# Neighbourhood attention's queries and keys projected in turned form and as two float32r parts, with the transposes one round later and two score tiles ahead of hyena's turns

## What is computed

```python
h = modulate_2(rmsnorm(x, g_mix), sh1, sc1)
z = h @ w_in[i]                                   # 256 x 3072
q, k, v = jnp.split(z[..., 3 * C_HYENA:], 3, axis=-1)   # 512 columns each, 16 heads of 32
hc = modulate_2(rmsnorm(xc, g_mix), csh1, csc1)   # the context, 256 tokens
kc, vc = jnp.split(hc @ w_in[i][:, kv_off:], 2, axis=-1)
y_na = neighborhood_attention(to_grid(q), to_grid(k), to_grid(v), kc, vc, na_rpb[i])
y_hy = hyena_mixer(z[..., :3 * C_HYENA], *hy)     # short filter, then two long convolutions
x = x + gt1 * (jnp.concatenate([y_hy, y_na], axis=-1) @ w_mix_out[i])
```

## Time and profile before

| what | value |
|---|---|
| runs | median 2493.89 us of 3, 2490.82 to 2494.59 |
| the profiled execution, its own time | 2489.44 us |
| its span | 2488.1 us |
| TensorE busy | 2369.3 us, 95% of the span |
| VectorE, ScalarE, GpSimd busy | 1788.6, 1223.7, 402.8 us |
| granted TensorE clock, mean | 0.968 of full |
| the projection (first L2491 to the end of L2497) | 898.7 to 1017.2 us |
| turns, attention and convolution | 1019.75 to 1152.9 us |

### The profile page before, as it was taken

How to read it: one execution, slowest core, us unless ns; L and a number is a source line. 1 busy time by engine, 2 the same in 40 slices (tenths; PEclk the granted TensorE clock), 3 DMA queues, 4 the chain that set the end, 5 groups by cost and what they waited for, 6 DMA issues and landing times.

```text
span 2488.1 us, 27394 instructions
## 1 busy us (share of the span) xinstructions
PE 2369.3 (95%) x10947; PEld 1770.0 (71%) x10949; DVE 1788.6 (72%) x2022; ACT 1223.7 (49%) x1441; POOL 402.8 (16%) x446
## 2 busy tenths in 40 slices
PE   6987999999999999899999989999999999999998
PEld 2455798544589875454997658778787788788886
DVE  4755577585688755455675358888888898889897
ACT  1132553223155321222443257676767777777775
POOL 1234470132247010253120000000000000000000
PEclk9988999997999999899999999999999999999999
DMA  7641478632447775104665339989998999899995
GB/s 306 252 180 51 179 275 314 225 147 109 159 179 263 306 297 201 76 6 164 236 221 203 146 139 354 363 326 367 349 368 317 367 344 369 318 363 357 363 355 217
DMA packets 50671, 630.35 MB, mean 253 GB/s; under 512 B 8695, under 2 KB 9384, under 8 KB 12840
## 3 DMA queue, kind: packets, MB, share of 16 engines
q1 hardware_dynamic: 44192, 618.81, 65.8%
q10 hardware_dynamic: 3960, 6.97, 0.9%
q0 software_dynamic: 2384, 2.73, 0.3%
HBM read 624.82 MB, written 3.67 MB: 253 GB/s over the span
## 4 chain that ended last, share of the span: by engine, by line
PE 81%; DVE 10%; DMA 3%; ACT 3%; issue 2%; POOL 1%; ACTq 0%; SPq 0%; DVEq 0%; POOLq 0%
PE psum L1136 18%; PE psum L1137 18%; PE psum L1138 18%; PE psum L1004 5%; PE psum L1031 4%; PE psum L2497 3%; DVE sbuf L701 2%; DVE ring_r L1131 2%; PE psum L2491 2%; DMA ring<-in_t_moe 2%; PE psum L741 1%; PE psum L1220 1%; PE psum L3110 1%; PE psum L1171 1%; DMA ring<-in_t_ada 1%
## 5 line engine op out<-in xcount | busy, mean ns | idle before, releaser
L1137 PE MATMUL psum<-ring_r,sc_r 128*128 128x512 f32 x1688 | 665.7, 394 | 0.0
L1131 DVE TENSOR_TENSOR ring_r<-ring,sbuf_r 128x2048 fp32r<-128x2048 f32 (+1 forms) x287 | 537.0, 1878 | 157.6 <-ACT sbuf_r L1122 156.0
L1122 ACT CAST sbuf_r<-ring 128x2048 fp32r<-128x2048 f32 (+1 forms) x287 | 444.9, 1556 | 327.1 <-PE psum L1138 252.2
L1131 DVE TENSOR_TENSOR ring_r<-ring,sc_r 128x2048 fp32r<-128x2048 f32 (+1 forms) x243 | 476.4, 1972 | 116.6 <-ACT sc_r L1122 116.0
L1122 ACT CAST sc_r<-ring 128x2048 fp32r<-128x2048 f32 (+1 forms) x243 | 397.3, 1642 | 255.6 <-PE psum L1138 216.2
L1136 PE MATMUL psum<-sbuf_r,sc_r 128*128 128x512 f32 (+1 forms) x1148 | 427.0, 372 | 4.5 <-DVE sc L2821 3.4
L1137 PEld LDWEIGHTS psum<-ring_r,sc_r 128*128 128x128 f32 x1688 | 317.3, 188 | 72.1 <-issue 1.4
L701 DVE SCALAR_TENSOR_TENSOR sbuf<-ring,sbuf 128x512 f32<-128x512 f32 x404 | 328.2, 819 | 20.5 <-DMA ring<-in_t_ada 15.0
L1138 PE MATMUL psum<-sbuf_r,sc_r 128*128 128x512 f32 x860 | 340.1, 395 | 0.0
L1136 PE MATMUL psum<-sc_r 128*128 128x512 f32 x828 | 330.9, 400 | 0.0
L1138 PE MATMUL psum<-sc_r 128*128 128x512 f32 x828 | 324.3, 392 | 0.0
(11 more groups left out here) (343 smaller groups left out, 2825.3 us busy)
## 6 DMA issues: line engine op xcount, KB each, us to landing
ring<-in_t_moe SPq DMA_DIRECT2D x168, 2048.0 KB, 7.9
ring<-in_t_ada SPq DMA_DIRECT2D x48, 2048.0 KB, 9.5
ring<-in_t_mlp SPq DMA_DIRECT2D x32, 2048.0 KB, 8.1
ring<-in_t_win SPq DMA_DIRECT2D x17, 2048.0 KB, 9.6
ring<-in_t_ffn SPq DMA_DIRECT2D x16, 2048.0 KB, 8.2
ring<-in_t_out SPq DMA_DIRECT2D x7, 2048.0 KB, 8.6
ring<-in_t_bias SPq DMA_DIRECT2D x2, 2048.0 KB, 10.0
spectra<-sc POOLq DMA_DIRECT2D x5, 512.0 KB, 3.9
```

The costliest lines, as they stand in the source:

```text
L1122: p.act.e.copy(p.r(hi), src).then_inc(*p.sig("high", st.tag, n))
L1131: p.dve.e.tensor_tensor(p.r(src), src, p.r(hi), ALU.subtract).then_inc(*p.sig("lowp", st.tag, n))
L1137: e.matmul(out, l[0], r[1], start=False, stop=False)
```

## The change

Queries and keys (units 6 to 11, tiles 3 and 4) are projected in turned form like hyena's columns, the context's keys too. `put_in2` splits each of these units into two float32r parts: ScalarE writes the rounded (and for queries scaled) part out of PSUM, then VectorE subtracts it from PSUM and writes the rest. The turns of queries and keys and the scaling on VectorE go. A score tile is now three float32r matmuls of 512 columns (high by high, high by low, low by high) where it was two float32 matmuls of 256. The depth of `Heads("na", ...)` goes from 2 to 3. The first two score tiles are made before hyena's turns; VectorE takes the first one's maximum before it copies hyena's turns, and ScalarE the first exponential behind its copies of them. Some buffers move. The loads of `skip` are issued behind the first exponential.

```diff
-        self.QA = v3(sc[:, 11288:12312], 4)
-        self.KA = v3(sc[:, 12312:13336], 4)
-        self.KC = v3(sc[:, 13336:14360], 4)
+
+        self.QAH, self.QAL = (v3(UQ[:, i, 0:1024], 4) for i in range(2))
+        self.KAL = [v3(self.GROW[3], 2), v3(sc[:, 13336:14360], 2)]
@@
-                             [(i,) for i in range(3)], [(3,), (4,)], 2)
+                             [(i,) for i in range(3)], [(3,), (4,)], 3)
@@
-                q = self.QA[r0:r0 + 32, h // 4, 128 * b:128 * b + 128]
-                na.job(h, [(q, self.KA[r0:r0 + 32, h // 4, :], 0, 256, True, True),
-                           (q, self.KC[r0:r0 + 32, h // 4, :], 256, 256, True, True)],
+                c = h // 4
+                qh, ql = (self.r(q[r0:r0 + 32, c, 128 * b:128 * b + 128]) for q in (self.QAH, self.QAL))
+                kh, kl = (self.r(k[r0:r0 + 32, :]) for k in (self.KAH[:, c, :], self.KAL[c // 2][:, c % 2, :]))
+                na.job(h, [(qh, kh, 0, 512, True, False), (qh, kl, 0, 512, False, False), (ql, kh, 0, 512, False, True)],
@@ def pe_in2
-            for c in range(2 if j < 3 else 1):
+            src = HT if i < 2 else p.HTC
+            for c in range(2 if j < 5 else 1):
                 for k in range(8):
...
+                    if j < 5:
+                        n = 256 * (i % 2) + 128 * c
+                        ins = e.matmul(ps[:, 256 * c:256 * c + 256], t[:, k, n:n + 128], src[:, k, :],
+                                       start=(k == 0), stop=(k == 7))
@@ def put_in2
+        if 6 <= u < 12:
+            hi, lo = in2_parts(p)[u - 6]
+            scale = 32 ** -0.5 if u < 8 else 1.0
+            ps = v3(p.bank[2 + u % 5], 2)
+            if side == "A":
+                E.wait_ge(*p.at("in2", u))
+                E.e.activation(p.r(hi), ps, ACT.Copy, scale=scale).then_inc(*p.sig("in2A", u))
+            else:
+                E.wait_ge(*p.at("in2A", u))
+                E.e.scalar_tensor_tensor(out=p.r(lo), in0=ps, scalar=scale, in1=p.r(hi), op0=ALU.mult,
+                                         op1=ALU.subtract).then_inc(*p.sig("in2D", u))
+            continue
@@ def pe_mix
+    for u in range(6, 12):
+        p.pe.wait_ge(*in2_at(p, u))
+    p.pe.wait_ge(*turn_at(p, "ctx", 2))
+    p.pe.wait_ge(*turn_at(p, "ctx", 3))
+    pe_scores(p, p.na, 0)
+    pe_scores(p, p.na, 1)
     p.pe.wait_ge(*p.at("short", 11))
...
-    pe_turn(p, "ka", lambda b, c: UQ[:, b, 512 + 128 * c:640 + 128 * c], 4, [0, 1])
...
-    pe_turn(p, "kc", lambda b, c: KVC[:, b, 128 * c:128 * c + 128], 4, [0, 1])
...
-    p.pe.wait_ge(*p.at("qscaled"))
-    pe_turn(p, "qa", lambda b, c: UQ[:, b, 128 * c:128 * c + 128], 4, [0, 1])
...
-        pe_round(p, p.na, one, two, end)
+        pe_round(p, p.na, one if i >= 2 else None, two, end)
@@ def act_mix
     put_hz(p, p.act, "A")
...
+    act_exp(p, p.na, 0)
@@ def dve_mix
+    dve_max(p, p.na, 0)
     put_hz(p, p.dve, "D")
...
+    dve_over(p, p.na, 0)
```

More of the change, by code:

```diff
@@ L213 @@
     "dve_once": ("condcopy", "posf", "vecs", "maskb", "latents", "lamsum", "shorts", "subln", "filterset", "ctxn",
-                 "edges", "qscaled", "second", "chosen", "placed", "flag", "turnedlogits"),
+                 "edges", "second", "chosen", "placed", "flag", "turnedlogits"),
     "act_once": ("silu", "latsq", "lamexp", "ctxsq", "secondexp", "keysA"),
@@ L325, in memory @@
         self.XNH = v3(wide[:, 0:2048], 2)
+        self.KAH = v3(wide[:, 0:2048], 4)
         small = region(1080)
@@ L532, in stages @@
         self.HZ = sc[:, 3072:6144].rearrange("p (b n) -> p b n", b=2)
-        self.QA = v3(sc[:, 11288:12312], 4)
-        self.KA = v3(sc[:, 12312:13336], 4)
-        self.KC = v3(sc[:, 13336:14360], 4)
+        self.QAH, self.QAL = (v3(UQ[:, i, 0:1024], 4) for i in range(2))
+        self.KAL = [v3(self.GROW[3], 2), v3(sc[:, 13336:14360], 2)]
         self.TM = v3(sc[:, 8216:9240], 2)
-        self.YF = [UQ[:, m // 2, 512 * (m % 2):512 * (m % 2) + 512] for m in range(4)]
+        self.YF = [sc[:, 11288 + 512 * m:11800 + 512 * m] for m in range(4)]
         self.SKIP = [KVC[:, o, 0:512] for o in range(2)]
         self.na = na = Heads("na", [sc[:, 6168 + 512 * i:6680 + 512 * i] for i in range(4)], [XN[:, i, :] for i in range(2)],
-                             [(i,) for i in range(3)], [(3,), (4,)], 2)
+                             [(i,) for i in range(3)], [(3,), (4,)], 3)
         for h in range(16):
@@ L2462, in in2_banks, with in2_parts @@
         out += [(p.ZT[:, 4 * j + 2 * c2:4 * j + 2 * c2 + 2, 1:257], True) for c2 in range(2)]
[L2463 to L2466, removed]
+    for high, low in in2_parts(p):
+        out.append((high, True))
+    out += [(p.UQ[:, b, 1024:1536], False) for b in range(2)]
+    out += [(p.KVC[:, b, 512:1024], False) for b in range(2)]
+    return out
+def in2_parts(p):
+    out = [(p.QAH[:, 2 * c:2 * c + 2, :], p.QAL[:, 2 * c:2 * c + 2, :]) for c in range(2)]
+    for n in (0, 256):
+        out += [(p.KAH[:, 2 * c:2 * c + 2, n:n + 256], p.KAL[c][:, :, n:n + 256]) for c in range(2)]
     return out
@@ L2473, in in2_at @@
 def in2_at(p, u):
-    return p.at("in2A" if u % 2 else "in2D", u)
+    return p.at("in2A" if u % 2 and not 6 <= u < 12 else "in2D", u)
 def pe_in2(p):
@@ L2486, in pe_in2 @@
             i = u - IN2_U[j]
-            for c in range(2 if j < 3 else 1):
+            src = HT if i < 2 else p.HTC
+            for c in range(2 if j < 5 else 1):
                 for k in range(8):
[L2489 to L2492, removed]
-                    else:
-                        if i >= 2:
-                            p.pe.wait_ge(*turn_at(p, "ctx", k // 2))
-                        src = HT if i < 2 else p.HTC
+                    p.pe.wait_ge(*(ht_at(p, 4, k) if i < 2 else turn_at(p, "ctx", k // 2)))
+                    if j < 5:
+                        n = 256 * (i % 2) + 128 * c
+                        ins = e.matmul(ps[:, 256 * c:256 * c + 256], t[:, k, n:n + 128], src[:, k, :],
+                                       start=(k == 0), stop=(k == 7))
+                    else:
                         ins = e.matmul(ps, src[:, k, 128 * (i % 2):128 * (i % 2) + 128], t[:, k, :],
@@ L2548, in pe_mix @@
         ins.then_inc(*p.sig("hzT", u))
-    p.pe.wait_ge(*turn_at(p, "ctx", 2))
-    p.pe.wait_ge(*turn_at(p, "ctx", 3))
-    pe_turn(p, "ka", lambda b, c: UQ[:, b, 512 + 128 * c:640 + 128 * c], 4, [0, 1])
-    p.pe.wait_ge(*turn_at(p, "ka", 0))
-    p.pe.wait_ge(*turn_at(p, "ka", 1))
-    pe_turn(p, "kc", lambda b, c: KVC[:, b, 128 * c:128 * c + 128], 4, [0, 1])
-    p.pe.wait_ge(*turn_at(p, "kc", 0))
-    p.pe.wait_ge(*turn_at(p, "kc", 1))
-    p.pe.wait_ge(*p.at("qscaled"))
-    pe_turn(p, "qa", lambda b, c: UQ[:, b, 128 * c:128 * c + 128], 4, [0, 1])
-    p.pe.wait_ge(*turn_at(p, "qa", 0))
-    p.pe.wait_ge(*turn_at(p, "qa", 1))
+    for u in range(12, 16):
+        p.pe.wait_ge(*in2_at(p, u))
     for u in range(1, 6):
@@ L2677, in act_mix @@
     for i, one, two, end in steps(p.na):
-        act_round(p, p.na, one, two, end)
+        act_round(p, p.na, one if i else None, two, end)
     act_turn(p, "hy", p.HT, 4, [0, 1])
@@ L2703, in dve_mix @@
                                        in1=p.ZC[:, c, :], op0=ALU.mult, op1=ALU.add).then_inc(*p.sig("short", c))
+    dve_max(p, p.na, 0)
     put_hz(p, p.dve, "D")
[L2705 to L2711, removed]
+    dve_over(p, p.na, 0)
     for i, one, two, end in steps(p.na):
-        dve_round(p, p.na, one, two, end)
+        dve_round(p, p.na, one if i else None, two, end)
         if i % 4 == 3 and i < 32:
```

## The result

| | before | changed |
|---|---|---|
| runs | 2489.95 us median of 20, 2481.93 to 2497.08 | 2501.10 us median of 20, 2493.34 to 2509.42 |
| the profiled execution | 2489.44 us | 2500.66 us |
| its span | 2488.1 us | 2499.4 us |
| TensorE's granted clock, mean | 0.968 | 0.965 |

The ratio of changed to before is 1.0049, with a 95% interval of 1.0039 to 1.0060: 12 us slower, by the medians 11. Forecast was slower by 7. That the time itself (2501) came out to the microsecond is luck: three runs had put the kernel before at 2493.89, 3.9 us above the 2489.95 of twenty, and the change was forecast some 4 us too small.

What follows compares the result with a forecast made beforehand. The prediction took TensorE to bound the kernel, by a narrow margin in the changed stage. Start -3.2, groups +4.6, tail +0.6 and clock +5 gave +7 us on 2493.9, so 2501 us; forecast's own range 2496 to 2508.

Steps and rivals of the forecast that it cites:

- The projection costs nothing: Input projection: the turned form costs TensorE nothing more and later VectorE products are covered; counted zero, 7 us without cover.
- The start, -3.2 us: Projection's end to first convolution step: turns removed, but the bias load delays the first maximum; -3.2 us, bounds -5.8 and -2.4.
- A score tile at 0.9 us: Neighbourhood attention's scores: three float32r matmuls of 512 columns take 0.9 us a tile, bounds 0.70 and 1.5.
- The groups, +4.6 us: Rounds between convolution steps: at depth 3 values products wait for ScalarE's copy behind the exponential; 14.4 and 15.5 us, +4.6.
- The tail, +0.6: Behind the last convolution step: three sets of transposes stand there rather than two, +0.6 us.
- The clock, +5: Seven intervals between steps: TensorE's longer stands bring one clock fall each, at 1.4 us; +5 us, bounds 0 and +10.
- The faster rival: Groups between steps: TensorE stays the bound, values products don't wait for ScalarE's copy; -8 us, 2486 us, chance 0.15.
- The no-change rival: Groups lengthen as worked out, but the clock does not fall more often; +2 us, 2496 us, chance 0.27.
- The much slower one: A 32-row score tile costs float32's rate, or the clock falls twice in some groups; 2505 to 2511 us, chance 0.10.

Runs made afterwards that it cites:

- the run with the copy first: Changed kernel, depth 3 kept, ScalarE's copy of the transposed probabilities put ahead of the exponential in neighbourhood attention: 2479.5 us, ratio 0.9954 to the kernel before.

## Why the forecast was right, and where it was off

**The projection costs nothing**: right. 118.5 us from the first L2503 to the bias load's issue, 118.55 before, though VectorE's products moved by a unit.

**The start, -3.2 us**: -4.2. The timeline shows each stop:

```profile
1017.91 0.80 SPq L3307 DMA_DIRECT2D ring<-in_t_bias  x2
...
1025.62 0.43 DVE L1241 TENSOR_TENSOR psum<-psum,ring 128x256 f32<-128x256 f32 x1 [7.71 <-DMA ring<-in_t_bias]
...
1027.43 0.66 PE L2574 MATMUL psum<-sbuf,sc 128*128 128x128 f32 x4 [1.25 <-DVE sc L2550]
...
1028.73 1.28 ACT L1274 ACT_TABLE_LOAD   x1
...
1032.72 1.12 PE L1196 MATMUL psum<-sbuf,sc 128*128 128x128 f32 x4 [0.23 <-POOL sc L1284]
...
1033.63 4.77 PE L2606 MATMUL psum<-sc,ring 128*128 128x512 f32 x8
```

VectorE idles 7.71 us until the bias tile lands, hyena's last turns follow, then the table load in the open. The stage is 0.7 us late as a whole; beyond that the first step's start (1032.6 forecast, 1033.8 measured) is 0.5 us late. The step itself was at half clock only until 1036.0 and took 4.57 us where 6.1 was taken, so that its end is 1.0 us early.

**A score tile at 0.9 us**: 0.91 on the chain. Within a tile the second matmul starts 0.34 us behind the first and the third 0.23 behind the second, so that with 32 rows the spacing of the earlier trace rows, taken with 128, is reached.

**The groups, +4.6 us**: the mechanism right, the size too small, and this is the largest part of what the forecast missed by. Clean intervals are 14.82 us, not 14.4, and by the distance of the two kinds of step (2.40 less 1.33) 15.9, not 15.5; no frequency interval was clean here. Over seven intervals less the first step, 104.4 us against 97.1: +7.3. The 0.4 us a group are small change that I had dropped: a step behind values takes 3.74 us until VectorE has it (I took 3.54 from a step behind transposes), each values product behind a wait 1.92 (I took 1.84 from one that had not waited), 0.02 us for the hop behind the tile. The row of a waiting product, 1.91, stood in the earlier trace rows.

**The tail, +0.6**: +0.9 (9.89 us from 1153.41 to 1163.30, against 8.95).

**The clock, +5**: +5.7. Seven stretches at half clock between first and last step, beginning at 1042.8, 1059.9, 1076.9, 1083.8, 1111.1, 1128.1 and 1135.0; seven were taken. They cost 115.0 less 104.4, so 1.5 us each. They did not come one to an interval: two of the seven had none and two had two. The rule of the Trainium skill, "TensorE: Matmul & The Clock Gate", section "A second HAM failure mode: psum-queue depth-cycling", that short pauses between groups make the clock swing, is borne out by this and by the run with the copy first, where pauses and falls went together; taken strictly, a fall in every group, it was not.

Sum by the trace: -4.2 + 7.3 + 0.9 + 5.7 = 9.7 us for the stage, which is 145.4 less 135.7. The profiled execution is 11.2 us longer than that of before; 0.7 lie ahead of the stage and 0.9 behind it, in parts that the change doesn't touch. So of the 4 us by which the forecast was too small, 2.7 are the groups, 1.6 lie outside the stage, 0.7 are the clock and 0.3 the tail, and the start takes 1.0 back. The turn at 1163.30, 10.35 us later, is just beyond the 5 to 10 given.

The faster rival is out by its own sign: values products wait up to 2.0 us for L1306. The no-change rival needed as many falls as before; there were seven for three. The much slower one needed a tile over 1.1 us, or two falls of the clock in some groups. Two groups did have two, but two had none, and seven in all was the number taken.

What no run tried: removing the falls of the clock with the stands kept. So their share is read from intervals with and without them, in one execution of each kernel, and the number of falls may differ in another.

## What to carry to other kernels

Where two engines pass work round in software-pipelined rounds, a greater depth moves each copy to another round, and so behind other waits of its engine's list: before changing the depth, write down for each queue what stands ahead of the instruction that the bottleneck waits for. Put short copies whose inputs are ready ahead of the step that waits for this round's own input. And cheaper work on the busiest engine buys little while a loop through the others closes at the same length (1 to 3 us for 15 here). Of two waits in one loop each gives a part alone (12 and 5 us), and only both together the whole (24).

## What the runs showed of the hardware that I had not expected

How much the clock adds to an ordering mistake. With the copy moved, the clean intervals would give 4 x 2.4 + 3 x 1.6 = 14 us (15.9 to 13.5 and 14.8 to 13.2); the run gained 24, since six of the seven falls of the clock between first and last step went with the stands. Standing more didn't lower the count either: the matmuls left out at depth 3 left TensorE at the low level for 37.5 us of the stage, where the changed kernel had 34.0 and the one with the copy first 10.2.
